# Conditioning chunks as float32 matmuls in four column groups of TensorE, columns taken by identity columns

## The reference

```python
mod = (silu(c) @ w_ada + b_ada).reshape(bsz, 1, 6, d)      # w_ada: 1024 x 6144
sh1, sc1, g1, sh2, sc2, g2 = (mod[:, :, i] for i in range(6))
h = x * (1 + sc1) + sh1
mix = token_mixer(h, ...)                # z = h @ w_in, cut into u, v and p
x = layer_norm(ALPHA * x + g1 * mix)
h = x * (1 + sc2) + sh2
x = layer_norm(ALPHA * x + g2 * moe(h))  # 32 experts, two per token
```

## Time and profile before

| | us |
|---|---|
| median of 3 runs | 1275.07 (1273.64 to 1277.22) |
| the profiled execution | 1272.6 |
| its span, first to last instruction | 1270.9 |
| TensorE busy | 1242.9 |
| VectorE, ScalarE, GpSimd busy | 948.9, 649.5, 195.6 |
| mean granted TensorE clock | 0.991 |

### The profile page before, as it was taken

How to read it: one execution, slowest core, us unless ns; L and a number is a source line. 1 busy time by engine, 2 the same in 40 slices (tenths; PEclk the granted TensorE clock), 3 DMA queues, 4 the chain that set the end, 5 groups by cost and what they waited for, 6 DMA issues and landing times.

```text
span 1270.9 us, 23452 instructions
## 1 busy us (share of the span) xinstructions
PE 1242.9 (98%) x6517; PEld 1021.2 (80%) x6518; DVE 948.9 (75%) x1160; ACT 649.5 (51%) x687; POOL 195.6 (15%) x257
## 2 busy tenths in 40 slices
PE   7999999999999998999999999999999999999897
PEld 6889999998888875788888888888888888888553
DVE  5767566456999989865798555754899888988497
ACT  5553222122222225665787555644778877787523
POOL 0011110000100111111122111111112212122122
PEclk8999999999999999999999999999999999999998
DMA  9944231016332568966999666865999999998993
GB/s 313 281 133 144 68 99 35 18 68 215 120 129 101 182 248 308 395 248 239 337 403 410 258 239 251 304 267 195 367 393 402 396 397 399 391 398 301 340 413 156
DMA packets 121934, 329.09 MB, mean 259 GB/s; under 512 B 12072, under 2 KB 43936, under 8 KB 121892
## 3 DMA queue, kind: packets, MB, share of 16 engines
q1 hardware_dynamic: 107700, 288.08, 60.6%
q0 software_dynamic: 12320, 34.15, 7.5%
q10 hardware_dynamic: 1872, 6.29, 1.2%
HBM read 296.97 MB, written 39.42 MB: 265 GB/s over the span
## 4 chain that ended last, share of the span: by engine, by line
PE 91%; DMA 3%; DVE 3%; SPq 2%; issue 1%; ACT 1%; POOL 0%; DVEq 0%; ACTq 0%; POOLq 0%
PE bank L1719 22%; PE bank L1721 22%; PE bank L1720 22%; PE bank L1732 3%; PE bank L1734 3%; PE bank L1733 3%; PE bank L2025 3%; DMA y<-y_rows 2%; PE bank L1942 1%; PE bank L2049 1%; PE bank L2120 1%; PE bank L2121 1%; PE bank L1782 1%; PE bank L1809 1%; PE bank L1773 1%
## 5 line engine op out<-in xcount | busy, mean ns | idle before, releaser
L1573 DVE TENSOR_TENSOR gu_l<-gu_raw,gu_h (+1 forms) x128 | 287.4, 2287 | 39.3 <-ACT gu_h L1031 28.4
L1719 PE MATMUL bank<-gu_h,xT_h 128*128 (+1 forms) x624 | 247.4, 396 | 1.8 <-DVE xT_l L1592 1.8
L1031 ACT ACTIVATE gu_h<-gu_raw (+1 forms) x128 | 239.1, 1928 | 10.3 <-issue 7.1
L1721 PE MATMUL bank<-gu_h,xT_l 128*128 (+1 forms) x624 | 243.8, 391 | 0.0
L1720 PE MATMUL bank<-gu_l,xT_h 128*128 (+1 forms) x624 | 243.3, 390 | 0.0
L1577 DVE TENSOR_TENSOR dn_l<-dn_raw,dn_h (+1 forms) x64 | 143.6, 2285 | 7.0 <-ACT dn_h L1035 4.4
L1719 PEld LDWEIGHTS bank<-gu_h,xT_h 128*128 128x128 f32 x624 | 117.6, 188 | 25.2 <-issue 1.7
L1721 PEld LDWEIGHTS bank<-gu_h,xT_l 128*128 128x128 f32 x624 | 117.5, 188 | 25.1
L1720 PEld LDWEIGHTS bank<-gu_l,xT_h 128*128 128x128 f32 x624 | 117.7, 189 | 23.3
L1719 PE MATMUL bank<-dn_h,aT_h 128*128 (+1 forms) x308 | 123.2, 400 | 0.0
L1721 PE MATMUL bank<-dn_h,aT_l 128*128 (+1 forms) x308 | 120.1, 390 | 0.0
(11 more groups left out here) (318 smaller groups left out, 2173.9 us busy)
## 6 DMA issues: line engine op xcount, KB each, us to landing
gu_raw<-in_w_gate_up SPq DMA_DIRECT2D x128, 1024.0 KB, 7.9
dn_raw<-in_w_down SPq DMA_DIRECT2D x64, 1024.0 KB, 7.5
y<-y_rows SPq DMA_DIRECT2D x22, 512.0 KB, 9.0
ada_raw<-in_w_ada SPq DMA_DIRECT2D x20, 512.0 KB, 7.3
ada_raw<-in_w_ada SPq DMA_DIRECT2D x10, 1024.0 KB, 5.3
win_raw<-in_w_in SPq DMA_DIRECT2D x8, 768.0 KB, 9.0
h_rows<-h SPq DMA_DIRECT2D x12, 512.0 KB, 2.6
fin<-x_rows SPq DMA_DIRECT2D x12, 512.0 KB, 11.2
```

Of the source, the lines that this page charges most:

```text
L1031: nc.scalar.activation(gu_slot(gu_h, e, c), gu_slot(gu_raw, e, c), ACT.Copy).then_inc(S["gu_split_h"], 1)
L1573: nv.tensor_tensor(gu_slot(gu_l, e, c), gu_slot(gu_raw, e, c), gu_slot(gu_h, e, c).bitcast(F32), ALU.subtract).then_inc(S["gu_split_l"], 1)
L1719: mm(out, lh, rh, start=start, stop=False)
L1721: return mm(out, ll, rh, start=False, stop=stop)
```

## The change

The split of the conditioning chunks is dropped: raw float32 blocks of w_ada go to TensorE as they are, against c_cols (float32, two columns, one per sequence). A chunk of 256 columns is taken as four parts of 64; part j is written to PSUM partitions 32j and 32j+1, so that each part has a column group of the array of its own: 32 float32 matmuls per chunk. ScalarE copies 98 partitions by 64 columns out in place of 4 by 256. The columns are made by two matmuls of that tile (98 rows, 64 columns) against four columns of the identity, which pick the rows 64c + 32a and 64c + 32a + 1. GpSimd adds a chunk to DRAM with four DMAs, one per part (two rows of 64 values each), all on one semaphore; before the adds of chunk n it waits for those of chunk n-2, and ScalarE before its copy of chunk n likewise, from n = 4 on. The buffers and steps of the split, c_hl and pair_sum go. The transpose of c and its copy move from bank 6 to bank 4, and the warm-up is 16 matmuls, eight each in banks 6 and 7, in place of 17 in bank 5.

```diff
-        ada0_raw, ada0_h, ada0_l = [], [], []
+        ada0_raw = []
...
+        late_rows = [Region(Z0 + (40 + s) * KB).take(f"late_rows{s}", [P, ADA_N // 4]) for s in range(2)]
...
+        open_rows = [Region(TOP0 + KB * s).take(f"open_rows{s}", [P, ADA_N // 4]) for s in range(2)]
...
-        mod_hl = [Region(r.at - 2 * KB + KB * s).take(f"mod_hl{s}", [4, ADA_N]) for s in range(2)]
+        mod_rows = [Region(r.at - 2 * KB + KB * s).take(f"mod_rows{s}", [P, ADA_N // 4]) for s in range(2)]
...
-            sp.wait_ge(S["added_l"], 16 * N_LATE)
+            for p in range(2):
+                sp.wait_ge(S[f"rows_added{p}"], 64 * (N_LATE // 2))
...
-            def add_low(n):
-                c = 2 * D + n * ADA_N
-                pool.wait_ge(S["added_h"], 16 * (n + 1))
-                nc.gpsimd.dma_start(mod_d[:, c:c + ADA_N], late_rows[n % 2][2:4, :], accum_op=ALU.add).then_inc(S["added_l"], 16)
-
             def add_rows(i, where):
                 if (i, where) in POINTS:
                     n = POINTS.index((i, where))
                     c = 2 * D + n * ADA_N
-                    if n >= 1:
-                        add_low(n - 1)
                     pool.wait_ge(S["late_row"], n + 1)
-                    nc.gpsimd.dma_start(mod_d[:, c:c + ADA_N], late_rows[n % 2][0:2, :], accum_op=ALU.add).then_inc(S["added_h"], 16)
+                    if n >= 2:
+                        pool.wait_ge(S[f"rows_added{n % 2}"], 64 * (n // 2))
+                    rows, w = (open_rows if n < N_OPEN else late_rows)[n % 2], ADA_N // 4
+                    for j in range(4):
+                        nc.gpsimd.dma_start(mod_d[:, c + j * w:c + (j + 1) * w], rows[32 * j:32 * j + 2, :], accum_op=ALU.add).then_inc(S[f"rows_added{n % 2}"], 16)
...
-            c_ps = ps[6][:, 0:2 * KD].rearrange("p (s k) -> p k s", s=2)
-            nc.scalar.activation(c_hl[:, :, 0:2], c_ps, ACT.Copy).then_inc(S["c_ready"], 1)
+            c_ps = ps[4][:, 0:2 * KD].rearrange("p (s k) -> p k s", s=2)
             nc.scalar.activation(c_cols[:], c_ps, ACT.Copy).then_inc(S["c_ready"], 1)
-
-            def high_first(m):
-                act.wait_ge((S["ada_first"], ada_loaded[0])[m], 16)
-                part = slice(m * P, (m + 1) * P)
-                nc.scalar.activation(ada0_h[0][:, :, part], ada0_raw[0][:, :, part], ACT.Copy).then_inc(S["ada_h_made"], 1)
...
-            def mod_hl_out(k):
+            def mod_row_out(k):
                 act.wait_ge(S["ada_made"], k + 1)
                 if k >= 2:
                     act.wait_ge(S["mod_cols"], k - 1)
-                nc.scalar.activation(mod_hl[k % 2][:], ps[6 + k % 2][0:4, 0:ADA_N], ACT.Copy).then_inc(S["mod_hl_made"], 1)
+                nc.scalar.activation(mod_rows[k % 2][0:98, :], ps[6 + k % 2][0:98, 0:ADA_N // 4], ACT.Copy).then_inc(S["mod_row"], 1)
...
-                nc.scalar.activation(late_rows[n][:], ps[6 + n][0:4, 0:ADA_N], ACT.Copy).then_inc(S["late_row"], 1)
-
-            mod_hl_out(0)
+                nc.scalar.activation(open_rows[n][0:98, :], ps[6 + n][0:98, 0:ADA_N // 4], ACT.Copy).then_inc(S["late_row"], 1)
...
-            def high_late(n):
-                act.wait_ge(ada_loaded[1 + late_slot(n)], 96 + 16 * sum(late_slot(m) == late_slot(n) for m in range(N_OPEN, n + 1)))
-                if n > N_OPEN:
-                    act.wait_ge(S["late_made"], n - N_OPEN)
-                nc.scalar.activation(ada_h[:], ada_raw[late_slot(n)][:], ACT.Copy).then_inc(S["late_h_made"], 1)
...
-                    act.wait_ge(S["added_l"], 16 * (n - 1))
-                    nc.scalar.activation(late_rows[n % 2][:], ps[POINT_BANK[where]][0:4, 0:ADA_N], ACT.Copy).then_inc(S["late_row"], 1)
+                    if n >= N_OPEN + 2:
+                        act.wait_ge(S[f"rows_added{n % 2}"], 64 * (n // 2))
+                    nc.scalar.activation(late_rows[n % 2][0:98, :], ps[POINT_BANK[where]][0:98, 0:ADA_N // 4], ACT.Copy).then_inc(S["late_row"], 1)
...
+                if i == NP - 1:
+                    for p in range(2):
+                        act.wait_ge(S[f"rows_added{p}"], 64 * (N_LATE // 2))
...
-            def low_ada0(k):
-                slot = k % ADA0_SLOTS
-                dve.wait_ge(S["ada_h_made"], k + 2)
-                nv.tensor_tensor(ada0_l[slot][:], ada0_raw[slot][:], ada0_h[k % 2][:].bitcast(F32), ALU.subtract).then_inc(S["ada_l_made"], 1)
...
-                pe.wait_ge(S["ada_l_made"], k + 2)
+                slot, w = k % ADA0_SLOTS, ADA_N // 4
+                if k == 0:
+                    pe.wait_ge(S["ada_first"], 16)
+                pe.wait_ge(ada_loaded[slot], 32 * (k // ADA0_SLOTS + 1) - (16 if slot == 0 else 0))
                 for kk in range(KD):
-                    mm(ps[6 + k % 2][0:4, 0:ADA_N], c_hl[:, kk, :], ada0_h[k % 2][:, kk, :], start=kk == 0, stop=False)
-                    last = mm(ps[6 + k % 2][0:4, 0:ADA_N], c_hl[:, kk, :], ada0_l[k % ADA0_SLOTS][:, kk, :], start=False, stop=kk == KD - 1)
+                    for j in range(4):
+                        last = mm(ps[6 + k % 2][32 * j:32 * j + 2, 0:w], c_cols[:, kk, :], ada0_raw[slot][:, kk, j * w:(j + 1) * w],
+                                  start=kk == 0, stop=kk == KD - 1)
                 last.then_inc(S["ada_made"], 1)
 
             def mod_columns(k):
-                pe.wait_ge(S["mod_hl_made"], k + 1)
-                for c in range(2):
-                    last = mm(ps[6 + k % 2][:, 2 * c:2 * c + 2], mod_hl[k % 2][:, c * P:(c + 1) * P], pair_sum[:], start=True, stop=True)
+                pe.wait_ge(S["mod_row"], k + 1)
+                for a in range(2):
+                    pick_rows = ident[0:98, :].rearrange("p (c a m) -> p a c m", c=2, a=2)[:, a, :, 0:2]
+                    last = mm(ps[6 + k % 2][64 * a:64 * (a + 1), 0:4], mod_rows[k % 2][0:98, :], pick_rows, start=True, stop=True)
                 last.then_inc(S["mod_cols"], 1)
...
-                    slot, out = late_slot(n), ps[POINT_BANK[where]][0:4, 0:ADA_N]
-                    pe.wait_ge(S["late_l_made"], n - N_OPEN + 1)
+                    slot, w = late_slot(n), ADA_N // 4
+                    pe.wait_ge(ada_loaded[1 + slot], 96 + 16 * sum(late_slot(m) == slot for m in range(N_OPEN, n + 1)))
                     for kk in range(KD):
-                        mm(out, c_hl[:, kk, :], ada_h[:, kk, :], start=kk == 0, stop=False)
-                        last = mm(out, c_hl[:, kk, :], ada_l[slot][:, kk, :], start=False, stop=kk == KD - 1)
+                        for j in range(4):
+                            last = mm(ps[POINT_BANK[where]][32 * j:32 * j + 2, 0:w], c_cols[:, kk, :], ada_raw[slot][:, kk, j * w:(j + 1) * w],
+                                      start=kk == 0, stop=kk == KD - 1)
                     last.then_inc(S["late_made"], 1)
...
-            nc.tensor.transpose(ps[6][:, 0:2 * KD], c_act[:], ident[0:2 * KD, 0:2 * KD]).then_inc(S["cT_made"], 1)
-            warm(5, 17)
-            pe.wait_ge(S["c_low"], 2)
+            nc.tensor.transpose(ps[4][:, 0:2 * KD], c_act[:], ident[0:2 * KD, 0:2 * KD]).then_inc(S["cT_made"], 1)
+            warm(6, 8)
+            warm(7, 8)
+            pe.wait_ge(S["c_ready"], 1)
             ada0_mm(0)
```

More of the change, by code:

```diff
@@ L175, in encoder @@
         r = Region(Z0 + 24 * KB)
-        ada_l = [Region(Z0 + (32 - 8 * s) * KB).take(f"ada_l{s}", [P, KD, ADA_N], F32R) for s in range(2)]
         ada_raw = [Region(Z0 + (32 - 8 * s) * KB).take(f"ada_raw{s}", [P, KD, ADA_N]) for s in range(2)]
-        ada_h = Region(Z0 + 40 * KB).take("ada_h", [P, KD, ADA_N], F32R)
+        late_rows = [Region(Z0 + (40 + s) * KB).take(f"late_rows{s}", [P, ADA_N // 4]) for s in range(2)]
         g2_raw = [Region(Z0 + 16 * KB * (s + 1)).take(f"g2_raw{s}", [P, KD, AW]) for s in range(2)]
@@ L197, in encoder @@
         c_cols = r.take("c_cols", [P, KD, 2])
-        late_rows = [Region(TOP0 + KB * s).take(f"late_rows{s}", [4, ADA_N]) for s in range(2)]
+        open_rows = [Region(TOP0 + KB * s).take(f"open_rows{s}", [P, ADA_N // 4]) for s in range(2)]
         r = Region(C1)
@@ L223, in encoder @@
         c_act = r.take("c_act", [2 * KD, P])
-        c_hl = r.take("c_hl", [P, KD, 4], F32R)
-        pair_sum = r.take("pair_sum", [4, 2])
         col_rows = r.take("col_rows", [NCOL, P])
@@ L752, in _ @@
                     add_rows(i, where)
-                    if (i, where) == POINTS[-1]:
-                        add_low(N_LATE - 1)
                 if i == NP - 1:
@@ L895, in _ @@
             copy_x0(2)
-            high_ada0(1)
             high_win(1)
-            high_ada0(2)
-            mod_hl_out(1)
+            mod_row_out(1)
             high_win(2)
@@ L903, in _ @@
                 if k + 1 < KD:
-                    mod_hl_out(k + 1)
+                    mod_row_out(k + 1)
                 else:
                     open_row(0)
-                if k + 2 < KD + N_OPEN:
-                    high_ada0(k + 2)
                 if k + 2 < KD:
                     high_win(k + 2)
```

(18 more changed lines are left out.)

43 lines of the change are left out of this document (4 added, 39 removed).

## The result

The changed kernel takes **1257.76 us** (median of 4 runs, 1257.11 to 1259.41), the kernel before, in the same session, 1275.01. The ratio is 0.9866, 95% interval 0.985 to 0.9881, so the gain is 17 us with an uncertainty of 2. The forecast was 1259.9 (15.2 us less). The profiled execution took 1257.66 us, its span is 1255.9; against the span before, 1270.9, that is 14.9 us less by the unrounded times.

What follows compares the result with a forecast made beforehand. DMA was taken to bound the kernel up to 30.5 us, TensorE afterwards. Gains of 8.5 us in the opening and 6.7 in late chunks made 15.2, so 1259.9 us against the median of 1275.1; range 1253 to 1277.

Steps and rivals of the forecast that it cites:

- What bounds the kernel: Whole kernel: DMA sets the pace up to 30.5 us; afterwards TensorE, busy 98% of the span, leads.
- Before 30.5 us: zero: Start of the opening: no gain, because DMA decides when u of k=1 starts; loss of 1, at most 3, if chunks cost 3.5.
- Part 1: Conditioning chunk on TensorE: 1.15 us in place of 1.82, between ends of 0.9 and 3.5 us.
- the upper end: Chunk on TensorE if the four column groups run one after another: 64 x 0.055 = 3.5 us.
- Part 2: Making columns by identity columns on TensorE: 0.25 us in place of 0.53, a gain of 0.28 per step.
- Part 3: ScalarE and VectorE relieved of splits: opening gains 8.5 us, 7.7 in six steps of 6.11 us, 0.8 in its end.
- Part 4: Ten late chunks on TensorE: 10 x (1.82 - 1.15) = 6.7 us gained, all on the path.
- Part 5: Adding rows by GpSimd, 48 small DMAs in place of 24: zero; eight issues take 6.4 us ahead of the first power().
- The sum: Whole kernel: 8.5 + 6.7 = 15.2 us gained, passed on whole behind 204 us; 1257.4 profiled, 1259.9 against the median.
- Starts every 24 to 30 ns: Rival on the chunk: starts, not columns, are the limit; chunk 1.55 to 1.9 us, time 1266 to 1272; 24%.
- No overlap: Rival on the chunk: four groups run in turn, chunk 3.5 us, together 25 us slower, 1300; 20%.
- The gain taken back: Rival: overlap works but a wait (GpSimd issue, DMA in the opening, gaps around chunks) replaces it; within 4 us of 1275; 8%.

## Why the prediction was right

**What bounds the kernel.** Right from 30.5 us on. Wrong in "up to 30.5 us the kernel waits for DMA". The transfer was the last link, but what waited for it was the copy of a block needed one step later, and hT_h(1), whose input was ready, stood behind it on ScalarE. "Before 30.5 us: zero" came out (30.54 for 30.51), for a reason that the run with the new order disproves: 25.01. In the kernel before, whose queues were fuller, the same order brought u of k=1 only to 29.30.

**Part 1, the chunk.** Taken at 1.15 us, and 1.15 is what a late chunk costs in place: 1.01 from its first record to the next instruction, and 0.15 more in what stands right before and behind it. The 0.25 us allowed for filling and emptying was the right size; more than half of it lies outside the chunk's own records, where "first to last record" doesn't look. That it came out to the hundredth is luck, since it was a choice between 0.9 and 3.5. The one-group run gives 3.67, so the upper end was right as well, if a little low. The rule of the Trainium skill (TensorE: Matmul & The Clock Gate, "Wait — 56ns, not 53.3ns?") that starts never come closer than about 25 ns does not hold across column groups: neighbours start 6 to 7 ns apart here. It would have given 1.6 us a chunk.

**Part 2, the columns.** Taken at 0.25 us; measured 0.21 for four records to the next start (0.28 to the end of the last), so 0.32 gained per step instead of 0.28.

**Part 3, the opening.** Forecast 8.5 us, measured 6.65. From k=2 to 6, five steps take 68.78 - 38.61 = 30.17 us, 6.03 each for 6.11 forecast, with no wait for hT_l, as said. (The bandwidth beside it was a little off: 1 MB and 768 KB are 1.84 million bytes, at 315 GB/s 5.8 us and not 5.6. It still fits, and no step waited for DMA.) The last part took 75.81 - 68.78 = 7.03 for 6.8, released by gelu, as said. What failed is the first step: 38.61 - 30.54 = 8.07 us in place of 6.11. Shorter chunks turned TensorE's work ahead of 30.5 us into idle time (5.04 us in place of 1.62 right before u), and the clock was half until 35.2 us. The forecast priced the start of u(1) and not the clock with which it would start. The relief of ScalarE and VectorE was counted only as the old waits, 0.58 us at every second step; by the run with the splits kept it is worth about 5 us, since the shorter chunk would have waited for the splits.

**Part 4, late chunks.** The stage gives 13.60 - 6.65 = 6.95 us for 6.7, all on the path, as said.

**Part 5, adding rows.** Zero was right. Eight issues took 6.83 us for 6.4.

**The sum.** 6.65 + 6.95 = 13.6 us for 15.2: the miss is the first step of the opening, 2 us of clock. The lead is still 13.54 in the routing stage (router at 463.50 for 477.04), 13.06 at the first expert block (482.96 for 496.02) and 14.64 at the third (512.45 for 527.09), because the kernel before loses 1.6 us to its clock episode there, while the one of the changed kernel cost it 0.5 at most in the routing stage. At the end it is 14.9. So 1.4 of the 14.9 us arose behind the stages that were changed, for the most part from where clock episodes fell, and not from any term of the forecast: that the profiled time is within 0.3 us of the forecast is luck, that it is near is not. The median fell by 17 because before it lay 2.4 us above its profiled execution, and after only 0.1.

**The rivals.** Starts every 24 to 30 ns: no, by the chunk in the trace and by the run with half the columns. No overlap: no; the one-group run shows what it would have cost. The gain taken back: only in the clock of the first step.

## What to carry to other kernels

Narrow matmuls with few weight columns and a long moving side belong in separate column groups: what is paid is about the columns of the longest group, and float32 without a split then costs less than the split with its copies on two other engines. Price such a burst together with what stands right before and behind it: the distance from its first record to the next instruction missed 0.14 of 1.15 us here. After such a relief, look at the order of the queues again: a copy for a later step that waits for a transfer should not stand ahead of work whose input is there, but the same order can lose when the queue is full. And don't shorten work that an engine does while it waits for others without looking at its granted clock.

## What the runs showed of the hardware

- Column groups of float32 matmuls with two weight columns overlap almost fully: 3.67, 1.84 and 1.01 us for the same columns in one, two and four groups, with starts of neighbouring groups 6 to 7 ns apart and starts in one group 55 ns apart. The section on packing small matmuls in the Trainium skill (TensorE: Matmul & The Clock Gate) measures 2.38 times for three column tiles; here it is 2.0 for two and 3.6 for four.
- Going into and out of such a burst cost TensorE about 0.15 us beside its own records: 0.21 us ahead of it in place of 0.12, and eight transposes in 0.85 us in place of 0.79.
- 128 records of half the columns took 1.17 us, 9 ns apart on average, where 64 took 1.01.
- The granted clock fell to 0.50 for 6.8 us where TensorE had idled 5.04 us, and from 457.5 to 471.2 us where it had been busy 1.83 of 2.50 us before. Episodes of 3.4 us come behind shorter idle times: at 472.1 us behind one of 1.80 us (from 468.9 to 470.7), in the kernel before at 514.4 behind waits of 0.60 and 1.50 us. The same two waits in the changed kernel (before 499.26 and 501.42) were followed by no drop; what decides stays open. The episodes move by tens of microseconds from one version to the next. One of 3.4 us cost 1.6 us among the expert blocks and 0.5 or less in the routing stage.
